# Two-block transformer forward: the first layer's modulation weights in groups of 6, 6, 4 and 8 slots, and the shared constants loaded later

## What is computed

```python
def modulation(cond, w, b):
    m = jax.nn.silu(cond) @ w + b
    return jnp.split(m, 3, axis=-1)
...
sh, sc, gt = modulation(c, ada_w[l], ada_b[l])
shc, scc, gtc = modulation(c_ctx, ada_w[l], ada_b[l])
h = rms_norm(x, norm_pre[l]) * (1.0 + sc[:, None]) + sh[:, None]
hc = rms_norm(xc, norm_pre[l]) * (1.0 + scc) + shc
z = h @ w_in[l]
zc = hc @ (w_in[l][:, :COL_Q] if last else w_in[l])
...
x_new = x + gt[:, None] * rms_norm(out, norm_post[l])
```

## Time and profile before

| | us |
|---|---|
| median of 3 executions | 1957.9 |
| lowest, highest | 1956.49, 1960.06 |
| the profiled execution | 1956.65 |
| its span in the profile | 1954.9 |
| TensorE, VectorE, ScalarE, GpSimd busy in the span | 1908.9, 1328.0, 995.1, 38.0 |

### The profile page before, as it was taken

The page is one execution under the profiler, slowest core; times in us unless marked ns, Lnnn a source line. Parts: engine busy times, 40 slices in busy tenths (PEclk is TensorE's granted clock), DMA queues, the critical chain, the costliest instruction groups (busy, mean ns, idle before and its releaser), DMA issues.

```text
span 1954.9 us, 26409 instructions
## 1 busy us (share of the span) xinstructions
PE 1908.9 (98%) x10944; PEld 1615.2 (83%) x10944; DVE 1328.0 (68%) x1806; ACT 995.1 (51%) x1450; POOL 38.0 (2%) x45
## 2 busy tenths in 40 slices
PE   6999999999999999999899999999999999999998
PEld 3899879899878898988788887788888888768886
DVE  5688788787788778865655566755566555686554
ACT  3465544465545455544544456554455444575444
POOL 1300000000000000000000000000000000000000
PEclk9999999999999999999999999999999999999999
DMA  9545676435675444465455554355555555525554
GB/s 369 197 146 189 216 239 194 148 122 192 214 246 187 172 130 131 161 212 184 130 189 188 187 178 143 129 193 185 191 173 181 186 189 188 172 87 183 188 189 140
DMA packets 95686, 353.73 MB, mean 181 GB/s; under 512 B 10640, under 2 KB 10768, under 8 KB 94800
## 3 DMA queue, kind: packets, MB, share of 16 engines
q1 hardware_dynamic: 90864, 331.12, 51.1%
q0 software_dynamic: 4416, 19.43, 2.9%
q10 hardware_dynamic: 288, 1.51, 0.2%
HBM read 350.97 MB, written 1.05 MB: 180 GB/s over the span
## 4 chain that ended last, share of the span: by engine, by line
PE 88%; DVE 7%; ACT 2%; DMA 2%; issue 1%; SPq 0%; DVEq 0%; ACTq 0%
PE PS L590 27%; PE PS L592 26%; PE PS L591 26%; DVE w_lo L1934 2%; DMA raw<-weights 2%; PE PS L767 1%; PE PS L1040 1%; ACT w_hi L1392 1%; PE PS L786 1%; PE PS L1003 1%; PE PS L871 1%; PE PS L1133 1%; PE PS L852 1%; PE PS L776 0%; PE PS L1122 0%
## 5 line engine op out<-in xcount | busy, mean ns | idle before, releaser
L1934 DVE TENSOR_TENSOR w_lo<-raw,w_hi 128x1024 fp32r<-128x1024 f32 x600 | 732.8, 1235 | 385.9 <-ACT w_hi L1392 384.5
L1392 ACT ACTIVATE w_hi<-raw 128x1024 fp32r<-128x1024 f32 x600 | 625.5, 1056 | 432.7 <-DMA raw<-weights 429.6
L590 PE MATMUL PS<-w_hi,h_hi 128*128 128x512 f32 (+1 forms) x1264 | 493.2, 390 | 7.8 <-DVE h_lo L2362 6.5
L592 PE MATMUL PS<-w_hi,h_lo 128*128 128x512 f32 (+1 forms) x1264 | 483.1, 382 | 0.0
L591 PE MATMUL PS<-w_lo,h_hi 128*128 128x512 f32 (+1 forms) x1264 | 482.6, 382 | 0.0
L590 PEld LDWEIGHTS PS<-w_hi,h_hi 128*128 128x128 f32 x1264 | 238.2, 188 | 59.3 <-issue 12.1
L590 PE MATMUL PS<-h_hi,w_hi 128*128 128x256 f32 x928 | 272.3, 293 | 5.0 <-DVE h_lo L1952 4.5
L592 PEld LDWEIGHTS PS<-w_hi,h_lo 128*128 128x128 f32 x1264 | 238.0, 188 | 46.6
L591 PEld LDWEIGHTS PS<-w_lo,h_hi 128*128 128x128 f32 x1264 | 238.5, 189 | 44.6 <-issue 1.4
L591 PE MATMUL PS<-h_lo,w_hi 128*128 128x256 f32 x928 | 264.2, 285 | 0.0
L592 PE MATMUL PS<-h_hi,w_lo 128*128 128x256 f32 x928 | 264.0, 284 | 0.0
(11 more groups left out here) (282 smaller groups left out, 1709.8 us busy)
## 6 DMA issues: line engine op xcount, KB each, us to landing
raw<-weights SPq DMA_DIRECT2D x614, 512.0 KB, 3.4
qk<-weights POOLq DMA_DIRECT2D x12, 512.0 KB, 4.8
v<-weights POOLq DMA_DIRECT2D x12, 512.0 KB, 5.6
x<-weights SPq DMA_DIRECT2D x6, 512.0 KB, 10.7
qk<-cond_in POOLq DMA_DIRECT2D x2, 1024.0 KB, 5.1
layer<-weights SPq DMA_DIRECT2D x3, 512.0 KB, 11.3
layer<-layer_in SPq DMA_DIRECT2D x1, 1536.0 KB, 6.8
layer<-layer_in POOLq DMA_DIRECT2D x1, 1536.0 KB, 8.4
```

The lines of the kernel that those rows point to most:

```text
L590: pe.matmul(dst, hi, m_hi_, start=first, stop=False, **kw)
L592: return pe.matmul(dst, lo, m_hi_, start=False, stop=last, **kw)
L1392: nc.scalar.activation(w_hi[:, r, :], raw[:, r, :], ACT.Copy).then_inc(w_hi_ready, 1)
L1934: V.tensor_tensor(w_lo[:, r, :], raw[:, r, :], f32(w_hi[:, r, :]), ALU.subtract).then_inc(w_lo_ready, 1)
```

## The change

The modulation's pieces go in groups of 3, 3, 2 and 4 (`ADA_PIECES`), so groups of 6, 6, 4 and 8 slots; 16 slots (shift and scale) are early and 8, the gate, late. The early slots start with the two halves of `x` in the rotation of buffers. The two more late slots go to the other half of `spec` for layer 1 and to scratch that the first norm uses; they are issued behind weight slot 5, the last when the norm's eight low halves are made. The constants are issued by GpSimd behind `spectrum_pairs(0)`. Behind the fourth pair, TensorE runs `late_modulation(3)`, `filter_energy(1)`, `ada_turn(3, 3)`, `filter_spectrum(1)`.

```diff
-ADA_TURN = 6
-ADA_TURNS = ADA_SLOTS // ADA_TURN
+ADA_PIECES = [3, 3, 2, 4]
+ADA_AT = [0, 3, 6, 8, 12]
+ADA_TURNS = len(ADA_PIECES)
-ADA_EARLY = ADA_SLOTS - ADA_TURN
+ADA_EARLY = 2 * ADA_AT[3]
+ADA_LATE = ADA_SLOTS - ADA_EARLY
...
-        ada_late += [spec[:, 1, 1, :, :].rearrange("p a c -> p (a c)")]
+        ada_late += [spec[:, 1, j, :, :].rearrange("p a c -> p (a c)") for j in range(2)]
+        ada_late += [scratch(7680, SLOT)]
...
+        def ada_buf(n):
+            return (n + RING) % ADA_BUFS
...
-                sp.dma_start(ada_raw[n % ADA_BUFS], weights[n]).then_inc(ada_loaded[n % ADA_BUFS], 16)
+                sp.dma_start(ada_raw[ada_buf(n)], weights[n]).then_inc(ada_loaded[ada_buf(n)], 16)
...
-                    sp.wait_ge(ada_used, max(m for m in range(ADA_EARLY) if m % ADA_BUFS == n) + 1)
+                    sp.wait_ge(ada_used, max(m for m in range(ADA_EARLY) if ada_buf(m) == n) + 1)
...
-                if 2 <= n < 5:
+                if 2 <= n < 6:
                     for j in (2 * (n - 2), 2 * (n - 2) + 1):
                         if j < 2:
-                            sp.wait_ge(ada_used, ADA_EARLY - 6 + j + 1)
+                            sp.wait_ge(ada_used, ADA_EARLY - 2 + j + 1)
+                        if j == ADA_LATE - 1:
+                            sp.wait_ge(norm_lo, KD)
                         sp.dma_start(ada_late[j], weights[ADA_EARLY + j]).then_inc(ada_late_loaded[j], 16)
...
-            pool.wait_ge(ada_used, 12)
-            pool.dma_start(consts[:, :], consts_in).then_inc(consts_loaded, 16)
...
             energy_sums(0)
             spectrum_pairs(0)
+            pool.dma_start(consts[:, :], consts_in).then_inc(consts_loaded, 16)
             energy_sums(1)
...
             modulation(2, 1)
-            modulation(2, 2)
             ada_turn(2, 1)
...
             def filters_and_gates(j):
                 if j == 0:
                     pe.wait_ge(rt_ready, 1)
-                if j < 3:
-                    late_modulation(j)
-                else:
+                late_modulation(j)
+                if j == 3:
+                    filter_energy(1)
                     ada_turn(3, 3)
-                    filter_energy(1)
                     filter_spectrum(1)
...
             def filters_and_gates(j):
-                if j < 3:
-                    ada_piece(3, j, (3, 3))
+                ada_piece(3, j, (3, 3))
```

More of the change, by code:

```diff
@@ L246, in build @@
         fconsts = scratch(5120, nfconsts)
-        ada_rows = scratch(1280, 3 * T)
+        ada_rows = scratch(1280, 4 * T)
         cond_rows = q[:, :, :].rearrange("p (w k) t -> p w (k t)", w=2)
@@ L309, in build @@
         ada_loaded = [sem(f"ada_loaded{j}") for j in range(ADA_BUFS)]
-        ada_late_loaded = [sem(f"ada_late_loaded{j}") for j in range(ADA_TURN)]
+        ada_late_loaded = [sem(f"ada_late_loaded{j}") for j in range(ADA_LATE)]
         ada_used = sem("ada_used")
@@ L674, in ada_turn @@
             def ada_turn(turn, bank):
-                pe.wait_ge(ada_rows_ready, 3 * turn + 3)
-                for j in range(6):
+                pe.wait_ge(ada_rows_ready, ADA_AT[turn + 1])
+                for j in range(2 * ADA_PIECES[turn]):
                     mm = pe.matmul(PS[:, bank, 2 * j:2 * j + 2], ada_rows[:, j * P:(j + 1) * P],
@@ L686, in modulation @@
                 if m == 2:
-                    pe.wait_ge(ada_rows_ready, 3 * turn + 1)
+                    pe.wait_ge(ada_rows_ready, ADA_AT[turn] + 1)
                 for half in range(2):
-                    n = ADA_TURN * turn + 2 * m + half
-                    pe.wait_ge(ada_loaded[n % ADA_BUFS], 16 * (n // ADA_BUFS + 1))
-                    ada_half(ada_raw[n % ADA_BUFS], m % 2, half).then_inc(ada_used, 1)
+                    n = 2 * (ADA_AT[turn] + m) + half
+                    pe.wait_ge(ada_loaded[ada_buf(n)], 16 * (n // ADA_BUFS + 1))
+                    ada_half(ada_raw[ada_buf(n)], m % 2, half).then_inc(ada_used, 1)
             def late_modulation(m):
                 if m >= 1:
-                    pe.wait_ge(ada_rows_ready, 3 * (ADA_TURNS - 1) + m)
+                    pe.wait_ge(ada_rows_ready, ADA_AT[3] + m)
                 for half in range(2):
@@ L1975, in ada_piece @@
             def ada_piece(turn, m, banks):
-                dve.wait_ge(ada_used, ADA_TURN * turn + 2 * m + 2)
+                dve.wait_ge(ada_used, 2 * (ADA_AT[turn] + m) + 2)
                 if m == 0 and turn > 0:
@@ L1983, in ada_take @@
                 dve.wait_ge(ada_turned, turn + 1)
-                V.tensor_copy(mod_raw[:, 12 * turn:12 * turn + 12], PS[:, bank, 0:12]).then_inc(ada_taken, 1)
+                a, b = 4 * ADA_AT[turn], 4 * ADA_AT[turn + 1]
+                V.tensor_copy(mod_raw[:, a:b], PS[:, bank, 0:b - a]).then_inc(ada_taken, 1)
             def modulation(turn, m):
```

## The result

The changed kernel took 1964.55 us (median of 7, 1959.54 to 1967.88) beside 1960.06 us for the one before (median of 7): ratio 1.0026, 95% interval 1.0014 to 1.0037. It is slower, by 4.5 us. The prediction was 1959.3 us with no measurable change as the likeliest outcome, and 1963.0 as the upper end.

What follows compares the result with a forecast made beforehand. TensorE was taken as the bound from the key and query projections on, with gains only in the first 48 us. Terms: -1.9 + 1.0 + 0.4 + 1.6 + 1.6 = +2.7 on 1956.65, 1959.3 us; range 1954.8 to 1963.0.

Steps and rivals of the forecast that it cites:

- The front, -1.9: Before the projections: weight tile 0's low half, then the fifth input tile, come 1.9 us earlier.
- the 4.9 us of the bytes: Front: if bytes set the time, two slots and the constants fewer gain 4.9 us; chance 0.13.
- the front's low stretches: TensorE's low clock at 34 to 35 and 49 to 50 us: left as is, 1.7 us either way.
- Added work, +1.0 and +0.4: TensorE, fourth projection pair: 16 small matmuls add 1.0 us, the last turn's 12 to 16 instructions 0.4 us.
- The new wait, +1.6: Last turn: TensorE stands 1.6 us for VectorE's copy of the fourth piece, behind two weight splits; bounds 0 and 2.0.
- The costless edits: Late slots ahead of weight tile 6 and constants issued at 57.54 us: lateness covered, 0 us.
- TensorE's clock, +1.6: Second filter's spectrum: low clock behind the idle time and last turn costs 1.6 us; ends 0 and 3.4.
- A low stretch like the first, laid over it: Second filter's spectrum: loses nearly the 1.7 us that the low clock cost at 30 to 40 us.
- the first rival: Second filter's spectrum: no low clock behind the stall, +1.1, 1957.8 us; chance 0.28.
- The 0.2%: Whole kernel: 0.2% (3.9 us) taken as what a measurement can tell from no change.
- the second rival: Front: bytes set it, gain 4.9 us; 1954.8 us (-1.9), or -3.5 without the stall; chance 0.13, 0.04 past 0.2%.
- The rival "slower": Front: first weight tile lands no earlier, front gain 0, +4.6, 1961.3 us; chance 0.14.

Runs made afterwards that it cites:

- the constants alone: Kernel before with only the constants' load moved behind the first filter's spectrum on GpSimd: 1958.21 us, ratio 1.0001.
- the groups alone: Changed kernel with the constants' load put back where it was, when 12 modulation slots are used: 1962.69 us, ratio 1.0025 to the kernel before.
- the second set of runs: Changed kernel measured once more without an edit: 1963.61 us against 1958.07 for the kernel before, ratio 1.0027.
- the stall filled: Changed kernel with two extra matmuls (1.4 us, results overwritten) between energy and last turn: 1960.04 us, ratio 1.0011 to the kernel before.
- the turn behind the spectrum: Changed kernel with the last turn moved behind the second filter's spectrum on TensorE: 1958.16 us, ratio 1.0001 to the kernel before.
- the copy early: Changed kernel with VectorE's copy of the fourth late piece ahead of its second weight split: 1958.98 us, ratio 1.0005 to the kernel before.
- the 14 matmuls in before: Kernel before with 14 extra matmuls in the gap ahead of the first projection's fifth input tile: 1957.69 us, ratio 0.9996.

## Why the prediction was right or wrong

*The front, -1.9.* Right in mechanism and size for the chain: tile 0's low half 1.7 us earlier, the fifth tile 1.7 to 2.0 us earlier in the change's three traces. It is not the 4.9 us of the bytes; that rival falls, and the constants alone (1.0001) show it best. At the first late modulation the mean gain is 1.6 us (54.27 against 52.66), and two of the three traces lost 3.4 us of clock around the fifth tile, where both traces of before lost 1.7 and the first trace of the change nothing. The prediction left the front's low stretches as they were, 1.7 either way; the traces bear that out. It named two of them, and its own trace has a third, at 0.50 from 18 to 21 us.

*Added work, +1.0 and +0.4.* The slots cost 1.0. The turn with four more instructions took 1.95 us in the full-clock trace against 1.39 in the same view of before: +0.6, not 0.4.

*The new wait, +1.6.* Right: 1.50, 1.49 and 1.50 us, at the place forecast, released by the copy behind two splits.

*The costless edits.* Right: the constants alone 1.0001, the groups alone as slow as the whole change, and no projection waits for tile 6.

*TensorE's clock, +1.6.* This step failed, by its size; that the low level would come behind the stall was right. "A low stretch like the first, laid over it" took one stretch of a single trace as the unit. In two of three traces the stretch behind the stall was twice as long, from within the turn to about a microsecond before the spectrum's end, and took 3.4 us. The step had named 3.4 as its upper end (for the spectrum alone) and not taken it. With 1.8, 3.4 and 3.4 the mean is 2.9, and the sum becomes -1.6 + 1.0 + 0.6 + 1.5 + 2.9 = +4.4 against the measured 4.5, and 5.5 in the second set of runs. Its terms are read from the traces after the fact, so this is an account and not a test; the test of the clock term is the stall filled, some 3 us. The Trainium skill (TensorE: Matmul & The Clock Gate, "HAM oscillation") tells of the throttled level behind waits longer than this stall. Read narrowly, as in the first rival, it gave no low level here (+1.1). The traces decide otherwise: the low level came in all three, behind 1.50, 1.49 and 1.50 us, and in the trace with the stall filled it did not.

*What the sum was made against.* This is the larger part of the miss in time. The forecast lay 5.2 us under the measured 1964.55; 1.8 of these are the change's effect (+2.7 against +4.5), and 3.4 the base. The profiled execution of before, 1956.65 us, was at the low end of its seven runs, whose median is 1960.06; the 33 later executions have a median of 1958.07. The text put the median 1.2 us higher and then gave the time on the lower base. With the right clock term and that base corrected, the forecast would have stood near 1962 to 1963. The range's upper end added only 1.7 us for the spread and should have taken the 3.4 of the clock with it. The 0.2% that was taken for what a measurement can tell was also too wide: seven runs of each kernel gave an interval of 0.0012 to either side, which tells the change's 0.26% from nothing. With that threshold the chances gave 0.81 to no measurable change, most of it to forecasts of +2.7 and +1.1 us. (The rivals' own chances add up to 0.82 and 0.04 where the text has 0.81 and 0.05, and the second rival's -3.5 us does not pass 3.9.) The rival "slower" ended at the measured size (+4.6) for a wrong reason: its tile that lands late never did.

## What to carry to other kernels

Work moved from the start into a stretch that TensorE bounds costs its own length and also needs its inputs from other engines there: find what the supplying engine has queued ahead, and put the consumer last in its group rather than ahead of dense work. An idle gap ahead of dense matmuls can cost more than itself (here 1.5 us and some 3 more by the clock), and that is seen in the mean over several traces and executions, not in one. Where a gap can't be closed, matmuls with unused results kept the clock behind the stall. In the front's gaps they raised the mean clock of the changed kernel (0.9914 to 0.9927 and 0.9942) and not that of the kernel before, and their gain in time was at the edge of what these runs can tell.

## What the runs showed that was not expected

The low level came in pieces of 1.7 or 3.4 us of lost clock, late in some traces of 5.1 (near 957 us), and in two traces (the turn behind the spectrum, the copy early) of 6.8 us in one stretch, from about 33 to 46 us, which took the first filter's spectrum from 3.68 to 6.5 us. Much of that was covered: TensorE had no gap left ahead of the fifth tile in these two traces, and the first late modulation started at 54.06 and 53.77 us, no later than in the kernel before. Over the whole span the three traces of the change lost 15.3, 20.6 and 20.1 us of clock, the two of before 15.5 and 15.6.

At the last turn, idle time of 1.5 us followed by two-column matmuls was followed by the low level in all four traces that have it; so was 0.37 us in the one trace with the copy early, and 0.21 us behind the filled stall was not. That is no rule. The second turn, in the front, stood 1.58 us in six traces, and the low level followed in four of them (the turn behind the spectrum, the copy early, the groups alone, the 14 matmuls in before). In the second trace of before and in the stall filled the granted clock stayed at 1.00 behind it, for over 12 us (its row in each of the two, in this order):

```profile
30.82 1.50 PE L678 MATMUL PS<-cols,arena 128*128 128x2 f32 x12 [1.58 <-DVE arena L1980]
30.54 1.50 PE L686 MATMUL PS<-cols,arena 128*128 128x2 f32 x12 [1.58 <-DVE arena L1988]
```

What else decides it, these runs do not show.
